# A decoder block on one core: the input product in passes over 512 features of h, with partial sums seeded back into PSUM

## The chip, the core and the metric

One core of a Trainium2 chip runs the whole kernel. The metric is the device time of one execution in microseconds (us), as the median of several runs. TensorE is PE in the profile, VectorE DVE, ScalarE ACT, GpSimd POOL; SyncE (SP) issues the DMAs.

## What is computed

One layer for 256 tokens (S) of 2,048 features (D), all in float32:

```python
mod = silu(c) @ w_ada + b_ada                      # 6 blocks of 2048: shift, scale, gate (mix), shift, scale, gate (ffn)
h = rmsnorm(x, g_pre_mix) * (1 + scale_m) + shift_m
z = h @ w_in                                       # q_lat, kv_lat, k_rope, gq, gk, gv, g_lr, g_og, gate_a, gate_b
y_a = mla_branch(...) @ w_branch_a                 # attention, 8 heads, latents up-projected, rope
y_b = gla_branch(...) @ w_branch_b                 # gated linear attention, 4 heads: a scan over tokens
merged = sigmoid(gate_a) * y_a + sigmoid(gate_b) * y_b
x = x + gate_m * rmsnorm(merged @ w_mix_out, g_post_mix)
h = rmsnorm(x, g_pre_ffn) * (1 + scale_f) + shift_f
x = x + gate_f * rmsnorm(conv_ffn(h), g_post_ffn)  # up to 2 x 5632, causal conv of width 3, gelu gate, down
```

The weights are 386 MB, read once. w_ada alone is 100 MB; the shift and scale of the first h are 4,096 of its 12,288 columns.

## The kernel before

**Numbers.** A float32 operand is split in a high part (float32r) and a low part, and a product is the sum of three matmuls: high x high, high x low, low x high. That holds for the weights and for h (`ht[:, k, 0]` and `[:, k, 1]`).

**Units, pairs, groups.** Weights come in *units* of 256 rows by 512 columns (512 KB, `raw`, a ring of 4). For each unit ScalarE makes the high half (`w_hi`, line 911), VectorE the low half (`w_lo`, line 1281), each one instruction of 128 x 1,024. TensorE takes two units at a time, a *pair*: 48 matmuls of 256 columns (`feature_pair`, lines 499 to 528) or 24 of 512. A *group* is 512 output columns: the pairs that sum over all of the rows (4 pairs for 2,048 rows) in two PSUM tiles (banks 0 to 3 rotate, `BANKS`), which ScalarE then copies out (`empty`, line 935). The list `GROUPS` (line 61) gives the order: misc (kv latent, rope, low-rank gate), qlat, gq x2, qup x3, kup, vup, gk x2, gv x4, og x4, ga x4, gb x4, ba x4, bb x4, mix x4, ffn x22, down x4, in all 530 units, 265 pairs, 133 of them before FFN.

**What sets the order.** Every engine's order is written out by hand; semaphores join them. ScalarE makes the high halves of pair k+2 once pair k is done (`pairs_used`, or `tile_ready` for the last pair of a group; `split_at`, line 922). The load of a unit waits on SP until the low half of the unit four back is made (line 314), and the one SP queue issues all of the loads in order.

**The modulation.** w_ada comes in units of 128 rows by 1,024 columns (512 KB, `ada`, a ring of 4). VectorE multiplies each by one column of silu(c) and adds it to `acc` (`ada_unit`, line 1284; 192 units in all). TensorE then sums `acc` over the partitions with a column of ones (`mod_columns`, line 567; for the first two blocks, lines 597 to 604). Shift and scale of the first h need 64 units; they run in two halves of 1,024 features (`first_ada`, lines 343 and 1362; `acc` and `acc_2`): after the first 32 units half of h is made (`input_hi`, line 968; `input_f` and `input_lo`, lines 1380 to 1391) and TensorE runs two pairs of misc, after the next 32 the rest. Then one unit of w_ada goes beside each pair, until the sixth block is done at the end of mix.

**Attention, scan.** From gk on, `mla_at` puts the pieces of a head of attention after the pairs, one head per two pairs (`scores`, `transpose_probs`, `context`); then come `gate_preact`, the decays (`log_gate`, `log_decay`) and 9 levels of the scan, one per two pairs: ScalarE's exponentials (`decays`, line 1079), VectorE's products (`products`, line 1520), TensorE's `level` (line 721), VectorE's masked copy (`select`, line 1528). GpSimd does the prefix sums (lines 1805 to 1814). The output of the scan (`gla_out`, `gla_norm_sum`) stands beside ga, one piece per pair. `gate_rows` (line 848) spreads the gate of the mix over all partitions after the last pair of ba; og_s, the split input of bb, is made when ba begins (lines 1150, 1618).

`pace` (line 495) is a small matmul ahead of a group.

Of the kernel before, what the change touches and what calls it, by code (L numbers as in the profile page):

```python
# [7 lines left out]
P = 128  # L8
# [52 lines left out]
GROUPS = ([("misc", 8, 2), ("qlat", 8, 2)] + [("gq", 8, 2)] * 2  # L61
          + [("qup", 2, 2)] * 3 + [("kup", 2, 4)] + [("vup", 2, 4)]
          + [("gk", 8, 2)] * 2 + [("gv", 8, 2)] * 4 + [("og", 8, 2)] * 4
          + [("ga", 8, 2)] * 4 + [("gb", 8, 2)] * 4 + [("ba", 4, 2)] * 4 + [("bb", 8, 2)] * 4
          + [("mix", 8, 2)] * 4 + [("ffn", 8, 2)] * 22 + [("down", 22, 2)] * 4)


def starts(name):

    u = t = p = 0  # L70
    a = 2 * ADA_BLOCK
    for kind, nu, nt in GROUPS:
        if kind == name:
            return u, t, p, a
        u, t, p = u + nu, t + nt, p + nu // 2 - 1
        if nu in (4, 8) and a < 6 * ADA_BLOCK:
            a += nu // 2
    return u, t, p, a


UNITS = starts("end")[0]
FIRST_OF = {g[0]: starts(g[0]) for g in GROUPS}


HALVES = {"mix": 0, "down": 8}
BANKS = 4

# [26 lines left out]
def build(nc, ap, out):  # L114
# [4 lines left out]
    with ctx:  # L119
# [41 lines left out]
        conv_a = at(5, "conv_a", [P, 4, S], F32, 4)  # L161
        conv_v = at(9, "conv_v", [P, 4, S], F32, 4)
# [9 lines left out]
        x_tok = at(B + 96, "x_tok", [P, NT, D], F32, 16)  # L172
        xn_tok = at(B + 112, "xn_tok", [P, NT, D], F32, 16)
        xn_t = at(B + 48, "xn_t", [P, KT, S], F32, 16)
        h_f = at(B + 64, "h_f", [P, KT, S], F32, 16)
# [8 lines left out]
        acc_2 = at(B + 128, "acc_2", [P, D], F32, 8)  # L184

        lat = at(B + 48, "lat", [P, 6, S], F32, 6)
        lat_s = at(B + 54, "lat_s", [P, 6, 2, S], F32R, 12)
        lat_sq = at(B + 66, "lat_sq", [P, 6, S], F32, 6)
        q_rope_in = at(B + 72, "q_rope_in", [P, 4, S], F32, 4)
        rope_tmp = at(B + 76, "rope_tmp", [P, 2, S], F32, 2)  # L190
        lat_r = at(B + 78, "lat_r", [P, 2, S], F32, 2)
# [11 lines left out]
        w_gate = at(B + 48, "w_gate", [P, GH * DK], F32, 4)  # L203
# [16 lines left out]
        brow_m = at(B + 128, "brow_m", [P, UC], F32, 2)  # L220
# [27 lines left out]
        tile_empty = sem("tile_empty")  # L248
        ada_used = sem("ada_used")
# [33 lines left out]

        def halves(t, h):
# [25 lines left out]
        def _(sp):  # L310
            def load_unit(u, r, src):
# [5 lines left out]
            def load_ada(a, r, src):  # L317

                if not isinstance(a, int) or a >= RING:
                    sp.wait_ge(ada_used, a - (RING - 1))  # L320
                sp.dma_start(ada[:, r], src).then_inc(ada_loaded[r], 16)

# [3 lines left out]
            def ada_src(block_no, kt, half):  # L326
                return w_ada[bass.ds(kt * P, P), bass.ds(block_no * D + half * AC, AC)]

            def group(u0, nu, src, a0=None, a_block=None, a_kt=None, slot0=0):

                for j in range(nu):
                    load_unit(u0 + j, (slot0 + j) % RING, src(j))
                    if a0 is not None and j % 2 == 1:
                        n = j // 2
                        load_ada(a0 + n, n % RING, ada_src(a_block, a_kt + n // 2, n % 2))

            def small(dst, src, loaded=rows_loaded):
                sp.dma_start(dst, src).then_inc(loaded, 16)

            def as_rows(v):  # L340
                return v.rearrange("(r c) -> r c", c=P)

            def first_ada(half, i):

                for r in range(RING):
                    a = 2 * KT * half + 4 * i + r
                    load_ada(a, r, ada_src(r % 2, 2 * i + r // 2, half))

            def load_misc(j):

                r = j % RING
                rs = w_in[j * 2 * P:(j + 1) * 2 * P, :].rearrange("(k p) n -> p k n", p=P)
                if j >= RING:
                    sp.wait_ge(lo_done, j - (RING - 1))
                sp.dma_start(raw[:, r, :, 0:320], rs[:, :, C_KV:C_KV + 320]).then_inc(raw_loaded[r], 16)
                sp.dma_start(raw[:, r, :, 320:384], rs[:, :, C_KR:C_KR + ROPE]).then_inc(raw_loaded[r], 16)
                sp.dma_start(raw[:, r, :, 384:512], rs[:, :, C_LR:C_LR + P]).then_inc(raw_loaded[r], 16)
# [7 lines left out]
            first_ada(0, 0)  # L365
            sp.dma_start(x_tok[:], x[0].rearrange("(t p) d -> p t d", p=P)).then_inc(x_loaded, 16)
# [9 lines left out]


            with sp.Fori(1, KT // 2) as i:
                first_ada(0, i)
            for j in range(RING):  # L380
                load_misc(j)
            with sp.Fori(0, KT // 2) as i:
                first_ada(1, i)
            _, _, _, a0 = FIRST_OF["misc"]
            for j in range(RING, 8):
                load_misc(j)
                if j >= RING + 1:
                    n = j - RING - 1
                    load_ada(a0 + n, n, ada_src(3, n // 2, n % 2))
            load_ada(a0 + 3, 3, ada_src(3, 1, 1))  # L390
            u0, _, _, a0 = FIRST_OF["qlat"]
            group(u0, 8, lambda j: two_kt(w_in, 256 * j, C_Q), a0, 3, 2)
            u0, _, _, a0 = FIRST_OF["gq"]
            with sp.Fori(0, 2) as g:
                group(u0 + 8 * g, 8, lambda j: two_kt(w_in, 256 * j, C_GQ + UC * g), a0 + 4 * g, 3, 4 + 2 * g)

            u0 = FIRST_OF["qup"][0]
            qv = w_q_up.rearrange("(k p) (h e) -> p k h e", p=P, e=NOPE + ROPE)
            for n in range(6):
                g, j = n // 2, n % 2  # L400
                r = (u0 + n) % RING
                sp.wait_ge(lo_done, u0 + n - (RING - 1))
                for k in range(2):
                    if g < 2:
                        dst = raw[:, r, k, :].rearrange("p (h e) -> p h e", h=4)
                        sp.dma_start(dst, qv[:, 2 * j + k, 4 * g:4 * g + 4, 0:NOPE]).then_inc(raw_loaded[r], 8 * 2)
                    else:
                        dst = raw[:, r, k, :].rearrange("p (h e) -> p h e", h=H)
                        sp.dma_start(dst, qv[:, 2 * j + k, :, NOPE:NOPE + ROPE]).then_inc(raw_loaded[r], 8 * 2)

            u0 = FIRST_OF["kup"][0]
            kvv = w_kv_up.rearrange("(k p) (h e) -> p k h e", p=P, e=NOPE + VD)
            for n in range(4):
                part, hh = n // 2, n % 2
                r = (u0 + n) % RING
                sp.wait_ge(lo_done, u0 + n - (RING - 1))
                for k in range(2):
                    dst = raw[:, r, k, :].rearrange("p (h e) -> p h e", h=4)
                    sp.dma_start(dst, kvv[:, k, 4 * hh:4 * hh + 4, part * NOPE:part * NOPE + P])\
                        .then_inc(raw_loaded[r], 16)  # L420
            s0 = FIRST_OF["gk"][0] % RING
            u0, _, _, a0 = FIRST_OF["gk"]
            with sp.Fori(0, 2) as g:
                group(u0 + 8 * g, 8, lambda j: two_kt(w_in, 256 * j, C_GK + UC * g), a0 + 4 * g, 3, 8 + 2 * g, s0)

            sp.wait_ge(tile_ready, FIRST_OF["gk"][1])
            sp.dma_start(w_gate[0:GR, :], w_gla_gate_up).then_inc(gate_w_loaded, 16)
            u0, _, _, a0 = FIRST_OF["gv"]
            with sp.Fori(0, 2) as g:
                group(u0 + 8 * g, 8, lambda j: two_kt(w_in, 256 * j, C_GV + UC * g), a0 + 4 * g, 3, 12 + 2 * g, s0)  # L430
# [11 lines left out]
            with sp.Fori(0, 2) as g:  # L442
                for n in range(2):
                    group(u0 + 8 * g + 4 * n, 4, lambda j: two_kt(w_branch_a, 256 * j, 2 * UC * g + UC * n),
                          None, None, None, s0)
                    for m in range(2):
                        load_ada(a0 + 4 * g + 2 * n + m, 2 * n + m, ada_src(2, 12 + 2 * g + n, m))
# [1389 lines left out]
```

## Time and profile before

| | us |
|---|---|
| median of three runs | 1787.48 |
| lowest and highest | 1781.24, 1788.38 |
| the profiled execution | 1779.35 |
| its span, from the first to the last instruction | 1777.6 |
| busy in it: PE, DVE, ACT, POOL | 1623.0, 1130.9, 749.6, 39.0 |
| mean DMA rate over the span | 219 GB/s |

PE's busy time is that of pipelined matmuls whose ends are modelled, so busy is not the same as at its peak. Times in rows are in us from the start of the span; a line of a timeline gives the start, the time that it took (for several of a kind, from the first to the last), engine, line of the kernel, operation and operands, and in brackets how long the engine had been idle and what ended that.

### The profile page before, as it was taken

The page shows a single profiled execution, that of the slowest core. Times are in us where ns is not written, and L with a number is a line of the kernel's source. Part 1 is how long each engine was busy: PE and PEld are TensorE (multiplying, and loading weights), DVE is VectorE, ACT ScalarE, POOL GpSimd, SP SyncE. Part 2 cuts the span into 40 slices and gives each one's busy share as a digit, 9 for nine tenths or more (in the row PEclk, how much of TensorE's full clock was granted, in tenths as well). Part 3 has the DMA queues.
Part 4 walks back from the last instruction along what each step waited for, and adds up shares of the span by engine and source line. Part 5 has one row for each costly group of instructions (what it writes and reads, how often), then busy time and mean ns, then how long its engine had stood idle before and what let it go on. Part 6 is the DMA issues. An engine that isn't in the chain of part 4 may idle for free.

```text
span 1777.6 us, 30678 instructions
## 1 busy us (share of the span) xinstructions
PE 1623.0 (91%) x11660; PEld 1509.6 (85%) x11660; DVE 1130.9 (64%) x1266; ACT 749.6 (42%) x921; POOL 39.0 (2%) x22
## 2 busy tenths in 40 slices
PE   1149999998998999998999789999999999999997
PEld 1149999787998999996988589999999999788886
DVE  6686756658775458684777756666666666544444
ACT  3114454435343454441443454455444455333332
POOL 0000000002220000000000000000000000000000
PEclk9569999998999999997999899999999999999999
DMA  8998867665565669983788636565566666555553
GB/s 310 330 308 294 235 217 233 229 214 185 172 212 178 213 214 297 298 289 134 265 314 294 226 112 192 187 192 190 189 189 191 195 193 195 170 190 190 190 191 138
DMA packets 188654, 389.15 MB, mean 219 GB/s; under 512 B 18445, under 2 KB 31503, under 8 KB 187815
## 3 DMA queue, kind: packets, MB, share of 16 engines
q1 hardware_dynamic: 188583, 388.17, 66.4%
q8 instruction: 48, 0.79, 0.2%
q14 instruction: 23, 0.19, 0.0%
HBM read 386.02 MB, written 2.10 MB: 218 GB/s over the span
## 4 chain that ended last, share of the span: by engine, by line
PE 81%; DVE 9%; DMA 4%; issue 3%; ACT 2%; SPq 1%; DVEq 0%; ACTq 0%
PE ps L519 17%; PE ps L521 17%; PE ps L523 17%; PE ps L558 6%; PE ps L560 6%; PE ps L559 6%; DMA ada<-in_w_ada 3%; DVE acc L1293 3%; DVE w_lo L1281 3%; PE ps L743 2%; ACT w_hi L911 1%; PE ps L795 1%; PE ps L797 1%; PE ps L796 1%; PE ps L855 1%
## 5 line engine op out<-in xcount | busy, mean ns | idle before, releaser
L1281 DVE TENSOR_TENSOR w_lo<-raw,w_hi 128x1024 fp32r<-128x1024 f32 x530 | 639.3, 1247 | 542.3 <-ACT w_hi L911 540.9
L911 ACT ACTIVATE w_hi<-raw 128x1024 fp32r<-128x1024 f32 x530 | 532.3, 1052 | 806.8 <-PE ps L523 521.9
L519 PE MATMUL ps<-h2t,w_hi 128*128 128x256 f32 x1408 | 390.7, 277 | 0.0
L523 PE MATMUL ps<-h2t,w_lo 128*128 128x256 f32 x1408 | 389.2, 276 | 0.0
L521 PE MATMUL ps<-h2t,w_hi 128*128 128x256 f32 x1408 | 389.1, 276 | 0.0
L519 PE MATMUL ps<-ht,w_hi 128*128 128x256 f32 x1152 | 329.4, 286 | 43.5 <-DVE ht L1391 40.1
L521 PE MATMUL ps<-ht,w_hi 128*128 128x256 f32 x1152 | 325.1, 282 | 0.0
L523 PE MATMUL ps<-ht,w_lo 128*128 128x256 f32 x1152 | 324.9, 282 | 0.0
L521 PEld LDWEIGHTS ps<-h2t,w_hi 128*128 128x128 f32 x1408 | 264.7, 188 | 0.0
L519 PEld LDWEIGHTS ps<-h2t,w_hi 128*128 128x128 f32 x1408 | 264.3, 188 | 0.0
L523 PEld LDWEIGHTS ps<-h2t,w_lo 128*128 128x128 f32 x1408 | 264.3, 188 | 0.0
L519 PEld LDWEIGHTS ps<-ht,w_hi 128*128 128x128 f32 x1152 | 223.5, 194 | 45.0 <-issue 41.0
L1293 DVE SCALAR_TENSOR_TENSOR acc<-ada,c_act,acc 128x1024 f32<-128x1024 f32 x182 | 234.1, 1293 | 19.9 <-DMA ada<-in_w_ada 19.0
L521 PEld LDWEIGHTS ps<-ht,w_hi 128*128 128x128 f32 x1152 | 223.1, 194 | 0.1
L523 PEld LDWEIGHTS ps<-ht,w_lo 128*128 128x128 f32 x1152 | 222.4, 193 | 0.0
L558 PE MATMUL ps<-w_hi,hid 128*128 128x512 f32 x352 | 138.8, 394 | 1.1 <-DVE w_lo L1281 1.1
L560 PE MATMUL ps<-w_hi,hid 128*128 128x512 f32 x352 | 137.8, 392 | 0.0
L559 PE MATMUL ps<-w_lo,hid 128*128 128x512 f32 x352 | 137.4, 390 | 0.0
L558 PEld LDWEIGHTS ps<-w_hi,hid 128*128 128x128 f32 x352 | 66.1, 188 | 16.2 <-DVE w_lo L1281 1.5
L560 PEld LDWEIGHTS ps<-w_hi,hid 128*128 128x128 f32 x352 | 66.1, 188 | 14.9
L559 PEld LDWEIGHTS ps<-w_lo,hid 128*128 128x128 f32 x352 | 66.1, 188 | 14.3
L519 PE MATMUL ps<-og_s,w_hi 128*128 128x256 f32 x256 | 72.7, 284 | 2.2 <-DVE w_lo L1281 2.2
(257 smaller groups left out, 1872.6 us busy)
## 6 DMA issues: line engine op xcount, KB each, us to landing
ada<-in_w_ada SPq DMA_DIRECT2D x192, 512.0 KB, 5.2
raw<-in_w_ffn_up SPq DMA_DIRECT2D x176, 512.0 KB, 4.5
raw<-in_w_in SPq DMA_DIRECT2D x168, 512.0 KB, 4.5
raw<-in_w_ffn_down SPq DMA_DIRECT2D x88, 512.0 KB, 3.8
raw<-in_w_branch_b SPq DMA_DIRECT2D x32, 512.0 KB, 5.5
raw<-in_w_mix_out SPq DMA_DIRECT2D x32, 512.0 KB, 5.5
raw<-in_w_branch_a SPq DMA_DIRECT2D x16, 512.0 KB, 5.9
raw<-in_w_q_up SPq DMA_DIRECT2D x12, 256.0 KB, 4.0
```

The source lines that it names most:

```text
L519: mm(o, w_hi[:, s, k, cols], moving[:, kt, 0], start=opens, stop=False, skip_group_check=True)
L521: mm(o, w_hi[:, s, k, cols], moving[:, kt, 1], start=False, stop=False, skip_group_check=True)
L523: ins = mm(o, w_lo[:, s, k, cols], moving[:, kt, 0], start=False, stop=stop, skip_group_check=True)
L558: mm(o, still[:, kt, 0, tok], w_hi[:, s, k, :], start=start, stop=False)
L559: mm(o, still[:, kt, 0, tok], w_lo[:, s, k, :], start=False, stop=False)
L560: ins = mm(o, still[:, kt, 1, tok], w_hi[:, s, k, :], start=False, stop=last and i == 1 and k == 1)
L743: ins = mm(o, lhs[:, d, keys], rhs, start=i == 0, stop=i == 1)
L795: mm(o, ht[:, kt, 0, tok], w_hi[:, s, k, :], start=first and i == 0 and k == 0, stop=False)
L796: mm(o, ht[:, kt, 0, tok], w_lo[:, s, k, :], start=False, stop=False)
L911: A(w_hi[:, slot], raw[:, slot], ACT.Copy).then_inc(hi_done, 1)
L1281: V.tensor_tensor(w_lo[:, slot], raw[:, slot], w_hi[:, slot].bitcast(F32), ALU.subtract)\
L1293: ins = V.scalar_tensor_tensor(part, ada[:, slot], c_act[:, bass.ds(kt, 1)], part, ALU.mult, ALU.add)
```

## The change

**Passes.** `PASSES` takes the place of `GROUPS`. The first 14 groups of w_in (FIRST: misc, qlat, gq, gq, gk; SECOND: gk, gv x4, og x4) no longer sum over all rows at once. One pass is one pair, 512 rows: all 14 over rows 0 to 511 (pairs 0 to 13), all 14 over rows 512 to 1,023 (14 to 27), then FIRST over rows 1,024 to 1,535 and 1,536 to 2,047 (28 to 37). After them come qup, kup, vup (38 to 42), and SECOND over its last 1,024 rows, two pairs a pass (43 to 60). From ga on (pair 61) the order is as before. The number of pairs is the same.

**Seeds.** At the end of a pass ScalarE copies the two tiles out to their place in SBUF as before. Ahead of the next pass over the same columns it copies them back into PSUM (`seed`), at the end of the pass two before, and the first matmul of that pass doesn't clear the bank (`opens` is false). TensorE waits for `seeded`.

**The modulation.** The first two blocks come in quarters: a unit is 128 rows by 512 columns of shift and the same of scale. 16 units make 512 features of h; TensorE starts pair 0 then. The other 48 units stand beside pairs 0 to 30, one or two each (`ada_schedule`), the columns and h's next quarter after pairs 11, 21 and 31. Blocks 2, 3, 4 follow beside pairs 33 to 51 and 65 to 77, 80 to 104, 106 to 130; block 5 beside the first eight FFN groups, through one slot. `acc_2` is gone.

**Attention and scan.** A head per pair from pair 43 (`MLA`), a level per pair from 57 (`GLA` is 55), the output of the scan from pair 65 (`OUT`), beside ga. The prefix sums are on VectorE (`scan`), in place of GpSimd. `gate_rows` comes after pair 79, columns of blocks 3 and 4 after 105 and 131. og_s is made after the last pair of ba (100). `pace` stays for gb, ba, bb and FFN, and is gone elsewhere.

The diff, cut:

```diff
+FIRST = [("misc", 0), ("qlat", 0), ("gq", 0), ("gq", 1), ("gk", 0)]
+SECOND = [("gk", 1)] + [("gv", g) for g in range(4)] + [("og", g) for g in range(4)]
+PASSES = ([(kind, g, 0, 2) for kind, g in FIRST + SECOND] + [(kind, g, 4, 2) for kind, g in FIRST + SECOND]
+          + [(kind, g, 8, 2) for kind, g in FIRST] + [(kind, g, 12, 2) for kind, g in FIRST]
+          + [("qup", g, 2, 2) for g in range(3)] + [("kup", 0, 0, 2), ("vup", 0, 0, 2)]
+          + [(kind, g, 8, 4) for kind, g in SECOND]
+          + [(kind, g, 0, 8) for kind in ("ga", "gb") for g in range(4)] + [("ba", g, 0, 4) for g in range(4)]
...
@@ SP @@
+            sp.dma_start(x_tok[:], x[0].rearrange("(t p) d -> p t d", p=P)).then_inc(x_loaded, 16)
+            for a in range(12):
+                load_ada(a)
+            load_pair(0)
+            for a in range(12, 16):
+                load_ada(a)
+            load_pair(1)
...
+            for k in range(FFN):
+                if k + 2 < FFN:
+                    load_pair(k + 2)
+                for n in range(ADA_AT[k]):
+                    load_ada(ADA_BEFORE[k] + n)
...
@@ PE @@
+                if seed is not None:
+                    pe.wait_ge(seeded, seed + 1)
+                elif not isinstance(t, int) or t >= 4:
                     pe.wait_ge(tile_empty, t - 3)
...
-                                opens = first and f == 0 and j == 0 and k == 0
+                                opens = first and seed is None and f == 0 and j == 0 and k == 0
...
+                if k in (11, 21, 31):
+                    first_columns((k - 1) // 10)
+                h = k - MLA
+                if 0 <= h < H:
+                    scores(h)
+                if 0 <= h - 3 < H:
+                    context(h - 3)
+                if 0 <= h - 2 < H:
+                    transpose_probs(h - 2)
...
+                if k == GLA:
+                    level(0)
+                if 1 <= k - GLA - 1 < LEVELS:
+                    level(k - GLA - 1)
...
@@ ACT @@
+            def seed(t, src):
+
+                act.wait_ge(tile_empty, t - 3)
+                A(as_tile(t, src), src, ACT.Copy).then_inc(seeded, 1)
...
+                else:
+                    split_pair(k + 2)
+                    if last and kind not in ("ba", "bb"):
...
+                        for b in range(2):
+                            empty(t0 + b, home(kind, g, b), ACT.Sigmoid if kind in ("ga", "gb") else ACT.Copy,
+                                  GLA_SCALE if kind == "gq" and k0 == 12 else 1.0)
+                        seed_pass(i + 2)
...
+                if kind == "ba" and g == 3 and last:
+                    act.wait_ge(og_gated, 4)
+                    act.wait_ge(tile_ready, first_tile("ba"))
+                    for q in range(4):
+                        A(og_s[:, 4 * q:4 * q + 4, 0], o_gla[:, 4 * q:4 * q + 4], ACT.Copy).then_inc(og_hi, 1)
...
@@ DVE @@
+            def scan(lv):
+
+                h = 1 << (lv - 1)
+                p0, p1 = halves(pre, h)
+                s0, _ = halves(suf, h)
+                dve.wait_ge(dec_ready, lv)
+                V.tensor_tensor(s0, s0, spread(p1[:, :, h - 1:h], s0), ALU.add).then_inc(suffix_ready, 1)
+                dve.wait_ge(suffix_ready, lv)
+                V.tensor_tensor(p1, p1, spread(p0[:, :, h - 1:h], p1), ALU.add).then_inc(scan_ready, 1)
...
+                if 1 <= k - GLA - 1 < LEVELS:
+                    select(k - GLA - 1)
+                if 1 <= k - GLA < LEVELS:
+                    if k - GLA < LEVELS - 1:
+                        scan(k - GLA)
+                    products(k - GLA)
...
+                for a in range(ADA_BEFORE[k], ADA_BEFORE[k] + ADA_AT[k]):
...
+                        ada_unit(a, a % RING, a % ADA_BLOCK // 2, a % 2, 16 * (a // RING + 1))
```

On VectorE these units come after the low halves and the small pieces of their pair, and ahead of the products of ba, bb and of og_s's low parts.

## Rows read from the trace of the kernel before

**Rows 1.** The page's 40 slices: TensorE's clock, then what the memory moved.

```profile
PEclk9569999998999999997999899999999999999999
GB/s 310 330 308 294 235 217 233 229 214 185 172 212 178 213 214 297 298 289 134 265 314 294 226 112 192 187 192 190 189 189 191 195 193 195 170 190 190 190 191 138
```

**Rows 2.** The page's chain of work that ended last, by engine.

```profile
PE 81%; DVE 9%; DMA 4%; issue 3%; ACT 2%; SPq 1%; DVEq 0%; ACTq 0%
```

**Rows 3.** Stretches: length, busy PE, PEld, DVE, ACT, POOL (count), clock, DMA share, GB/s.

```profile
640.00:760.00 120.00, 120.00 (x1060) 120.00 (x1060) 92.25 (x78) 56.96 (x60) 0.00 (x0) 1.00 0.87 286
1034.00:1512.00 478.00, 478.00 (x4202) 478.00 (x4202) 302.06 (x388) 238.10 (x304) 0.00 (x0) 1.00 0.60 189
```

**Rows 4.** Timeline of VectorE in the first 136 us.

```profile
37.49 2.67 DVE L1293 SCALAR_TENSOR_TENSOR acc<-ada,c_act,acc 128x1024 f32<-128x1024 f32 x2 [0.44 <-DMA ada<-in_w_ada]
...
125.49 1.28 DVE L1293 SCALAR_TENSOR_TENSOR acc<-ada,c_act,acc 128x1024 f32<-128x1024 f32 x1 [0.89 <-DMA ada<-in_w_ada]
...
134.39 1.23 DVE L1391 TENSOR_TENSOR ht<-h_f,ht 128x1024 fp32r<-128x1024 f32 x1 [0.72 <-ACT ht L973]
```

**Rows 5.** Timeline, TensorE's first matmul on h.

```profile
103.36 0.55 PE L519 MATMUL ps<-ht,w_hi 128*128 128x256 f32 x1 [29.98 <-DVE ht L1391]
```

**Rows 6.** Timeline of ScalarE: high halves, each pair of them behind a pair of TensorE.

```profile
143.23 2.01 ACT L911 ACTIVATE w_hi<-raw 128x1024 fp32r<-128x1024 f32 x2 [5.01 <-PE ps L523]
...
290.17 2.01 ACT L911 ACTIVATE w_hi<-raw 128x1024 fp32r<-128x1024 f32 x2 [1.08 <-PE ps L523]
...
304.36 2.01 ACT L911 ACTIVATE w_hi<-raw 128x1024 fp32r<-128x1024 f32 x2 [1.08 <-PE ps L523]
...
469.35 2.01 ACT L911 ACTIVATE w_hi<-raw 128x1024 fp32r<-128x1024 f32 x2 [6.76 <-PE ps L523]
...
484.93 2.01 ACT L911 ACTIVATE w_hi<-raw 128x1024 fp32r<-128x1024 f32 x2 [8.13 <-PE ps L523]
...
559.25 2.00 ACT L911 ACTIVATE w_hi<-raw 128x1024 fp32r<-128x1024 f32 x2 [5.01 <-PE ps L523]
...
574.03 2.01 ACT L911 ACTIVATE w_hi<-raw 128x1024 fp32r<-128x1024 f32 x2 [5.92 <-PE ps L523]
...
805.28 2.00 ACT L911 ACTIVATE w_hi<-raw 128x1024 fp32r<-128x1024 f32 x2 [3.43 <-PE ps L523]
...
834.84 2.01 ACT L911 ACTIVATE w_hi<-raw 128x1024 fp32r<-128x1024 f32 x2 [27.56 <-PE ps L523]
```

**Rows 7.** Chain in order of time: mod_columns, a selection, a level, gate rows twice.

```profile
367.08 3.47 PE ps L573 x32
...
474.00 1.23 DVE attn L1551 x8
475.37 3.76 PE ps L743 x32
...
810.07 2.05 PE ps L853 x2
...
1515.85 1.05 PE ps L855 x2
```

**Rows 8.** Groups by line and shape: count | busy us, mean ns | idle before.

```profile
L911 ACT ACTIVATE w_hi<-raw 128x1024 fp32r<-128x1024 f32 x530 | 532.3, 1052 | 806.8 <-PE ps L523 521.9 <-PE ps L560 185.3 <-DMA raw<-in_w_in 58.6
L939 ACT ACTIVATE k_gla<-ps 128x512 f32<-128x512 f32 x4 | 2.1, 584 | 0.0
L1281 DVE TENSOR_TENSOR w_lo<-raw,w_hi 128x1024 fp32r<-128x1024 f32 x530 | 639.3, 1247 | 542.3 <-ACT w_hi L911 540.9
```

**Rows 9.** Timeline of VectorE, two low halves while GpSimd scans.

```profile
439.50 5.29 DVE L1281 TENSOR_TENSOR w_lo<-raw,w_hi 128x1024 fp32r<-128x1024 f32 x2
```

**Rows 10.** DMA issues from 650 to 800 us: count, KB each, us to landing.

```profile
raw<-in_w_in SPq DMA_DIRECT2D x34, 512.0 KB, 4.9
```

More of the change, by code:

```diff
@@ new lines, in numbers @@
+def numbers():
+    first, tiles, seeds, pairs = [], [], [], []
+    t = p = n = 0
+    for i, (kind, g, k0, nu) in enumerate(PASSES):
+        nt = 4 if kind in ("kup", "vup") else 2
+        first.append((t, p))
+        seeded = k0 > 0 and kind != "qup"
+        seeds.append(n if seeded else None)
+        n += nt if seeded else 0
+        for m in range(nu // 2):
+            last = m == nu // 2 - 1
+            pairs.append((i, m, ("tile_ready", t + nt) if last else ("pairs_used", p + m + 1)))
+        t, p = t + nt, p + nu // 2 - 1
+        tiles.append(nt)
+    return first, tiles, seeds, pairs
@@ L85, with at_pair, first_tile @@
+START, TILES, SEEDS, PAIRS = numbers()
+def at_pair(kind, g=0, k0=None):
+    return next(k for k, (i, m, _) in enumerate(PAIRS)
+                if PASSES[i][:2] == (kind, g) and m == 0 and (k0 is None or PASSES[i][2] == k0))
+def first_tile(kind):
+    return START[PAIRS[at_pair(kind)][0]][0]
+UNITS = 2 * len(PAIRS)
+LAT = at_pair("qlat", 0, 12)
+MLA = at_pair("gk", 1, 8)
+GLA = MLA + 12
+OUT = MLA + 22
+ROWS = OUT + 14
+FFN = at_pair("ffn")
 HALVES = {"mix": 0, "down": 8}
 BANKS = 4
+GATE_BANKS = ((7, 4), (6, 5))
@@ new lines, in ada_schedule @@
+def ada_schedule():
+    n = [0] * FFN
+    for k in range(31):
+        n[k] = 2 if k % 2 == 0 or k == 15 else 1
+    for k in list(range(33, MLA + 9)) + list(range(OUT, ROWS - 1)):
+        n[k] = 1
+    for k in list(range(ROWS + 1, ROWS + 25)) + list(range(ROWS + 27, ROWS + 51)):
+        n[k] = 2 if k % 3 == 0 else 1
+    assert sum(n[:31]) == 48 and sum(n[31:ROWS]) == 32
+    assert sum(n[ROWS:ROWS + 25]) == 32 and sum(n[ROWS + 25:]) == 32
+    return n
+ADA_AT = ada_schedule()
+ADA_BEFORE = [16 + sum(ADA_AT[:k]) for k in range(FFN)]
@@ L89, in level_masks @@
+MOD_3 = ROWS + 26
+MOD_4 = FFN - 2
 def level_masks():
@@ L329, in group @@
[L329 to L357, printed above, removed]
+            qv = w_q_up.rearrange("(k p) (h e) -> p k h e", p=P, e=NOPE + ROPE)
@@ L390, in _ @@
[L390 to L409, printed above, removed]
@@ L439, in _ @@
-            sp.wait_ge(og_psum, 8)
-            sp.dma_start(gpost_m[:], g_post_mix[0:1, :].to_broadcast([P, D])).then_inc(post_loaded, 16)
-            u0, _, _, a0 = FIRST_OF["ba"]
[L442 to L447, printed above, removed]
@@ new lines, in _, with ffn_loads @@
+            u0, a0 = 2 * FFN, 5 * ADA_BLOCK
+            def ffn_loads(g, with_ada):
+                for part in range(2):
+                    for j in range(8):
+                        load_unit(u0 + 16 * g + 8 * part + j, (u0 + j) % RING,
+                                  two_kt(w_ffn_up, 256 * j, part * FF + UC * g))
+                        if with_ada and j in (3, 7):
+                            n = 2 * part + j // 4
+                            sp.wait_ge(ada_used, a0 + 4 * g + n)
+                            sp.dma_start(ada[:, 3], w_ada[bass.ds((2 * g + n // 2) * P, P), bass.ds(5 * D + n % 2 * AC, AC)])\
+                                .then_inc(ada_loaded[3], 16)
```

1247 lines of the change are left out of this document (541 added, 706 removed).

## The prediction

> **What bounds the kernel now.** I read the page's slices first, for the places where TensorE falls behind. TensorE runs at full clock from about 150 us on; in the first slices it is nearly idle at half clock, while the memory moves 290 to 330 GB/s [rows 1]. The chain agrees: 81% of it is TensorE, and the 4% of DMA and much of the 9% of VectorE lie at the start [rows 2]. The table by stretches gives the price of steady work: FFN's 88 pairs of units (two units, 48 matmuls of 256 columns) take 478 us, so **a pair costs 5.44 us** with TensorE never idle, and w_in's gate columns run at the same pace while 286 GB/s come in [rows 3]. So the kernel is 265 pairs of TensorE time plus what lies between them, and a change pays only in what lies between.
>
> The timeline of VectorE tells what the start is: it sums shift and scale columns as w_ada lands, the 16th unit being used by 40.2 us, the 64th by 126.8 us; then come the columns on TensorE and the split of h, whose low part ends at 135.6 us [rows 4]. TensorE's first two pairs ran at 103 to 111 and 118 to 124 us, after 30 us of nothing [rows 5]. ScalarE's high halves are a clock of the pairs, as each pair of them waits for the pair of units before last: pair 2 ended at 143.2 us [rows 6], 3 x 5.44 back is 126.9 us, the point from which the pairs would have run without a gap.
>
> **The start.** After the change 16 units of w_ada make the first 512 features of h, not 64. The same bytes have landed by then as at 40.2 us before, plus pair 0's 1 MB put in between (3.4 us at 310 GB/s, between slices of rows 1), in pieces of 2 KB where they were 4 KB, for which I add 1 us: the last of the 16 is used at 44.5 us. From 126.8 to 135.6 us the same tail took 8.8 us before; it has half of the columns now (16 of 32 instructions), so at half clock, where 32 take twice the 3.47 us of [rows 7], less 2 us and some: 7 us. TensorE starts at 51.7 us. The pair that starts cold took 7.6 us (135.6 to 143.2), I say 8: pair 0 ends at 59.8 us, and 5.44 back is 54.4. **Gain 126.9 - 54.4 = 72.5 us**, between 66 (two stalls of the ring) and 75.
>
> **Loads beside the first 31 pairs.** They carry 48 more units of w_ada: per pair 1.05 MB of weights and 1.55 x 0.52 MB, 1.86 MB, which at 5.44 us is 342 GB/s. The columns stretch moved 286 GB/s at a share of 0.87 [rows 3], so 329 at a full share, and 1.86 MB takes 5.66 us: 31 x 0.22 = 7 us. If it only reaches the 310 of the slices it is 31 x 0.56 = 17; if the stretch's share understates what is left, 0. **Cost 7 us.** The Trainium skill, page DMA: Bandwidth & Descriptors, section Specifications, gives HBM a limit of about 358 GB/s per core; by that figure the pair would stay at 5.44 us and this cost would be nothing. The trace has slices of 330 and none above, so its row is kept.
>
> **ScalarE beside those pairs.** A pass is one pair now: two high halves (2 x 1.05), two evictions (2 x 0.58) and two seeds [rows 8]. No row shows a copy into PSUM; the nearest are the eviction's 0.58 us for 512 elements and half of a 1.05 us copy of 1,024: I take 0.58; twice that is the dear bound. Sum 4.4 us, 5.6 us at the dear bound: under, or 0.1 over, the pair. As pass i seeds for i+2, one pair of TensorE covers it. VectorE has two low halves (2 x 1.25) and 1.55 sums (1.28): 4.5 us. **Nothing**, dear bound 5 us. Behind them on both queues are the chunks of h (four ScalarE pieces, two VectorE steps, three times): they have one to three pairs of cover. The three new sets of columns stand on TensorE's path: 16 instructions, 1.7 us each: **cost 5 us**.
>
> **Latents.** The chain from root to low part had a whole group of four pairs; it has two, and VectorE has splits and a sum ahead of its part. Nothing to one pair: **cost 3.5 us**.
>
> **Attention and scan beside one pair each.** A head had two pairs and cost 14.2 - 10.9 = 3.3 us (304.36 less 290.17 in [rows 6]); with one pair the round is 5.44 + 3.3 = 8.7 us, and no other engine has more than 7 us in it (VectorE: 2.5, 1.3 and some 2.7 of small pieces). Same cost. A level took 15.6 us in two pairs (484.93 less 469.35), 4.7 above them. Now: level 3.76 us, selection 1.23 us [rows 7], two scan steps and two products of 1,024 elements at 1.25 us, 5 us, all in a ring: 10.0 us, some 10.2 with semaphores, against 9.2 of TensorE: 4.8 above the pair; on ScalarE every second pair has evictions and seeds ahead of the decays, 1 us more in three or four levels. **Cost 4 us**, bounds 0 and 20. The scan leaves GpSimd; while it ran there, two low halves took 5.29 us against 2 x 1.25 [rows 8, 9], a delay that goes. The entry to the scan (gate, log, first decays: a long serial piece) keeps its length and I leave it equal.
>
> **Later.** (a) First output of the scan: 559.25 to 574.03 is 14.8 us [rows 6], a pair plus 1.4 is 6.8: the wait for the last selection has a pair of cover now, **gain 8**. (b) Gate rows: 805.28 to 834.84 us holds one pair and 24.1 us [rows 6]; 4.8 were a wait for the sums and eight steps ran at 2.05, which at full clock take 1.05 (the second such set) [rows 7]. Moved among the gate columns, with sums done two pairs ahead: 8.4 us, **gain 15.5**, at least 7.7 if at half clock. (c) og_s is split only after the last branch-a pair. Behind that pair: first high half, two low halves, one sum, two gate products (half of 1.25 each), one low part: 1.05 + 2.5 + 1.3 + 1.3 + 1.25 = 7.4 us, in which TensorE waits; then half clock for a while, 4; before, that place lost 1.3. **Cost 10**, bounds 6 and 15. (d) w_ada's last block beside FFN: two sums per four pairs (21.8 us) for VectorE, busy 302 of 478 us: nothing; if they delayed one split per group, 11 us. (e) A pace matmul and a rope wait less: gain 2.
>
> **Sum**: 72.5 - 7 - 5 - 3.5 - 4 + 8 + 15.5 - 10 + 2 = 68.5 us. The profiled execution took 1779.35 us (span 1777.6): 1710.9. The median of three is 1787.5, 8 above it; I put half of that on top: **1714 us**.
>
> **Rivals.** (1) *Loads and ScalarE bind more*: the first stage's period is 6.4 to 7 us, or the scan's ring 12 to 13: 25 to 45 us less gain, 1740 to 1760. For it: every copy is now serial behind a pair; against: margins of 1 us above. Chance 0.2. (2) *Slower*: landing time. Pair k+2 is issued when pair k's low halves are made, 2 periods less 3.5 us before it is due; w_ada's queue turns behind it in the same in-order queue. Landing took 4.9 us at 290 GB/s [rows 10]; 7.4 us decide whether there is a loss, and from (L + 3.5)/2 = 7.7 us, L = 11.9, the change is slower. With L = 14: 8.75 us, 31 x 3.3 = 103 us, 1806 us. 0.05. (3) *The clock falls in single-pair passes*. From 440 us on TensorE changed banks and waited a little each level and the slices show 9 tenths or more [rows 1]. The Trainium skill, TensorE: Matmul & The Clock Gate, section A second HAM failure mode, says that cycling through PSUM banks with micro-idles makes the clock swing. As a mechanism of this kernel, with half of 31 pairs at half clock: 15 x 5.44 = 82 us, 1796: no change. 0.03. (4) *The start is not where the time is*: x's own chain (norm, transposes) ends after the 16th unit. x is now first in the queue, so it would have to lose 10 us: 1724, inside the range. The forecast has the rest, 0.72.
>
> **Numbers.** The range takes in the forecast with its bounds (1695 to 1735) and most of rival 1: 1692 to 1758. About 0.5% is what a measurement of this kernel tells from no change. Faster 0.92, the same 0.03, slower 0.05.
>
> **What would show it.** First TensorE pair near 52 us; high halves every 5.5 to 5.8 us up to 230 us, with the memory above 310 GB/s; heads every 8.7, levels every 10.2; gate rows in 8.4 us; one wait of 7 us at the first branch-b matmul; FFN unchanged at 478 us. A wait of TensorE on ScalarE's copies into PSUM in the first stage, or a period above 6.5 us there, would prove the forecast wrong.

## The result and the profile after

The changed kernel takes 1824.1 us (median of four runs, 1819.4 to 1831.3) against 1785.7 us before on the same chip: a ratio of 1.022, 95% interval 1.018 to 1.026. It is 2.2% slower where 1714 us was forecast. The profiled execution, the slowest of the four, took 1831.27 us; its span is 1829.5 us.

The page of the kernel after, slices and chain (the lines that answer to [rows 1, 2]):

```profile
PEclk8899999998999899899979898989898999999999
GB/s 290 274 326 337 322 236 228 219 153 93 109 207 246 178 318 312 228 247 344 324 160 116 173 171 197 165 210 148 197 171 173 191 187 195 163 193 192 194 187 138
...
PE 71%; DVE 9%; DMA 7%; issue 5%; ACT 5%; SPq 1%; DVEq 0%; ACTq 0%
PE ps L544 14%; PE ps L546 14%; PE ps L548 14%; PE ps L573 7%; PE ps L571 7%; PE ps L572 7%; DMA raw<-in_w_ffn_up 6%; ACT w_hi L890 3%; DVE w_lo L1232 3%; PE ps L730 2%; DVE acc L1266 2%; DVE acc L1255 1%; DMA ada<-in_w_ada 1%; DVE conv_v L1626 1%; DVE hid_f L1639 1%
```

TensorE's share of the chain fell by ten points, and a DMA stands in it that was not there: the landing of w_ffn_up's raw units, 6% of the span, some 110 us. At the start the clock's slices read 8 and 8 where they read 5 and 6. New are five dips, in every second slice from the 23rd to the 31st, which lie in FFN; the kernel before has none there.

Where the time went is told by TensorE's first and last matmul of FFN. The trace's group of `w_lo` matmuls on `h2t`, of the kernel before and then of the one after (name, count, duration min/median/max in ns, first and last start in us):

```profile
L523 PE MATMUL ps<-h2t,w_lo x1408: 276/276/286, 1033.1 to 1514.7; 128*128 128x256 f32 x176
```

```profile
L548 PE MATMUL ps<-h2t,w_lo x1408: 276/276/416, 964.5 to 1565.7; 128*128 128x256 f32 x176
```

FFN begins 68.6 us earlier and lasts 601.2 us where it lasted 481.6: 119.6 us more. Behind it the two are alike (262.9 us to the end of the span before, 263.8 after). So -68.6 + 119.6 + 0.9 = +51.9, which is the difference of the spans. The forecast's sum, 68.5 us, is there at the door of FFN; all of the miss is inside.

FFN as a whole, before and then after (columns as in [rows 3]):

```profile
1032.80:1514.80 482.00, 482.00 (x4235) 482.00 (x4236) 304.29 (x390) 239.21 (x305) 0.00 (x0) 1.00 0.59 188
```

```profile
964.20:1565.80 601.60, 525.55 (x4235) 522.15 (x4236) 342.84 (x422) 242.96 (x305) 0.00 (x0) 0.93 0.52 178
```

For the same 4,235 matmuls TensorE is busy 43.6 us longer, at a clock of 0.93, and idle for 76.0 us: that is the whole of the 119.6.

Two stretches inside (the first lies in the eight groups with w_ada's last block, the second is mostly the three groups without it):

```profile
965.00:1432.00 467.00, 390.95 (x3076) 387.55 (x3075) 257.25 (x313) 177.57 (x222) 0.00 (x0) 0.91 0.50 175
1432.00:1550.00 118.00, 118.00 (x1016) 118.00 (x1017) 76.05 (x99) 57.90 (x76) 0.00 (x0) 0.98 0.60 188
```

Without w_ada FFN keeps the old pace. With it, TensorE idles 76 of 467 us at a clock of 0.91, and every other engine is less busy than before too, the memory with them (175 GB/s, share 0.50, against 189 and 0.60 in [rows 3]): nobody works at a limit, somebody waits. Who, the trace's waits of that stretch show, TensorE's, ScalarE's, VectorE's and SyncE's queue (who waited <- for what: us in total, times, longest):

```profile
PE ps L544 <- DVE w_lo L1232: 42.4, 9, 6.1
PE ps L522 <- DVE w_lo L1232: 33.6, 8, 4.8
...
ACT w_hi L890 <- DMA raw<-in_w_ffn_up: 158.6, 51, 9.7
...
DVE w_lo L1232 <- ACT w_hi L890: 201.7, 55, 8.2
...
SPq L482 <- DVE acc L1266: 379.4, 31, 33.1
```

Read backwards: TensorE waits for low halves, 17 times; VectorE for high halves; ScalarE for the raw units to land; and the queue that issues the raw units stands 379 of 467 us in front of one semaphore, "the previous unit of w_ada has been summed" (line 481, then the DMA of line 482). The timeline of SyncE's queue shows it as bunches:

```profile
980.17 0.34 SPq L482 DMA_DIRECT2D ada<-in_w_ada  x1
980.77 2.23 SPq L371 DMA_DIRECT2D raw<-in_w_ffn_up  x4
991.82 0.35 SPq L482 DMA_DIRECT2D ada<-in_w_ada  x1
992.41 2.23 SPq L371 DMA_DIRECT2D raw<-in_w_ffn_up  x4
1008.65 0.35 SPq L482 DMA_DIRECT2D ada<-in_w_ada  x1
1009.56 2.24 SPq L371 DMA_DIRECT2D raw<-in_w_ffn_up  x4
```

Four raw units are issued at once each time, and only when a sum is done. The chain at the first of these:

```profile
978.73 1.29 DVE acc L1266
980.17 0.34 SPq L482
980.77 0.37 SPq L371
981.39 6.71 DMA raw<-in_w_ffn_up
988.11 1.06 ACT w_hi L890
989.20 1.24 DVE w_lo L1232
990.44 0.12 issue
990.56 0.58 PE ps L544
991.13 0.21 PE ps L546
```

From the end of the sum (980.0) to the landing at 988.1 no unit is in the ring: the ring of four has run dry. TensorE still has its last pair until 986.2; then it idles for 4.35 us, until the new unit has landed and been split (990.6). Its matmuls then come every 0.21 us, which is half clock; from 994.1 on they come every 0.12 us again.

**Theory A** from these rows. In a group of 16 units VectorE sums behind units 7, 9, 15 and 17 (`j in (5, 7)` of both parts; 17 is unit 1 of the next group). SyncE loads w_ada behind raw units 3, 7, 11 and 15, always into slot 3, and each load waits for the sum before it. The load behind raw unit 7 needs the sum that stands behind the low half of unit 7 (and 15 that of 15). Raw units 8 to 11 stand behind it in the same queue, though their own slots (those of 4 to 7) come free one by one from unit 4 on. So twice in each of eight groups all four slots run empty. 119.6 / 16 = 7.5 us each: 4.75 us of waiting (76.0 us, in 17 recorded waits) and 2.7 us of slower matmuls. **Rivals**: B, VectorE overfull with the sums; C, the added transfers make the units land late; D, a loss of pace that has nothing to do with w_ada. (The expectations say 107 us: they took FFN to end at 1550, before I had the last matmul's row. The right figure is 119.6.)

### The profile page after: what moved, and what is told of

It is laid out like the page before. It is cut to its first block, busy times and chain, and to the rows that moved or that the text cites. A ratio compares the mean times of both kernels' runs of the same rounds, so it can differ in the third digit from the quotient of the medians.

```text
span 1829.5 us, 29229 instructions
## 1 busy us (share of the span) xinstructions
PE 1658.2 (91%) x11650; PEld 1548.2 (85%) x11650; DVE 1131.3 (62%) x1285; ACT 819.7 (45%) x1053; POOL 3.7 (0%) x9
## 4 chain that ended last, share of the span: by engine, by line
PE 71%; DVE 9%; DMA 7%; issue 5%; ACT 5%; SPq 1%; DVEq 0%; ACTq 0%
PE ps L544 14%; PE ps L546 14%; PE ps L548 14%; PE ps L573 7%; PE ps L571 7%; PE ps L572 7%; DMA raw<-in_w_ffn_up 6%; ACT w_hi L890 3%; DVE w_lo L1232 3%; PE ps L730 2%; DVE acc L1266 2%; DVE acc L1255 1%; DMA ada<-in_w_ada 1%; DVE conv_v L1626 1%; DVE hid_f L1639 1%
## 5 line engine op out<-in xcount | busy, mean ns | idle before, releaser
L1232 DVE TENSOR_TENSOR w_lo<-raw,w_hi 128x1024 fp32r<-128x1024 f32 x530 | 627.1, 1222 | 615.6 <-ACT w_hi L890 614.0
L544 PE MATMUL ps<-h2t,w_hi 128*128 128x256 f32 x1408 | 409.9, 291 | 42.4 <-DVE w_lo L1232 42.4
L546 PE MATMUL ps<-h2t,w_hi 128*128 128x256 f32 x1408 | 406.1, 288 | 0.0
L548 PE MATMUL ps<-h2t,w_lo 128*128 128x256 f32 x1408 | 405.4, 288 | 0.0
L544 PEld LDWEIGHTS ps<-h2t,w_hi 128*128 128x128 f32 x1408 | 281.1, 200 | 44.2 <-issue 43.4
L546 PEld LDWEIGHTS ps<-h2t,w_hi 128*128 128x128 f32 x1408 | 281.4, 200 | 0.0
L548 PEld LDWEIGHTS ps<-h2t,w_lo 128*128 128x128 f32 x1408 | 280.3, 199 | 0.0
```

Of the source, the lines that this page charges most:

```text
L544: mm(o, w_hi[:, s, k, cols], moving[:, kt, 0], start=opens, stop=False, skip_group_check=True)
L546: mm(o, w_hi[:, s, k, cols], moving[:, kt, 1], start=False, stop=False, skip_group_check=True)
L548: ins = mm(o, w_lo[:, s, k, cols], moving[:, kt, 0], start=False, stop=stop, skip_group_check=True)
L1232: V.tensor_tensor(w_lo[:, slot], raw[:, slot], w_hi[:, slot].bitcast(F32), ALU.subtract)\
```

## Experiments on FFN

The kernel before ran beside every experiment, at 1791 to 1792.5 us in the median where it had 1785.7 beside the first runs; the ratios to it are the safer figures.

**Without the block.**

```diff
-                        if with_ada and j in (3, 7):
-                            n = 2 * part + j // 4
-                            sp.wait_ge(ada_used, a0 + 4 * g + n)
-                            sp.dma_start(ada[:, 3], w_ada[bass.ds((2 * g + n // 2) * P, P), bass.ds(5 * D + n % 2 * AC, AC)])\
-                                .then_inc(ada_loaded[3], 16)
...
-                        if with_ada and j in (5, 7):
-                            n = 2 * part + (j - 5) // 2
-                            ada_unit(a0 + 4 * g + n, 3, 2 * g + n // 2, n % 2, 16 * (a0 // RING + 4 * g + n + 1))
...
-            gate_rows(6 * ADA_BLOCK, brow_f)
+            gate_rows(5 * ADA_BLOCK, brow_f)
```

> Leaves out w_ada's last block beside FFN altogether: its 32 loads and its 32 sums, so the gate row of FFN is made of the bias alone. The time it gives is that of the kernel after without this work. Changed kernel: 1824 us median, FFN 965 to 1550 us. Every theory that puts the 107 us into this block (A: SyncE's in-order queue stands behind the one-slot buffer; B: VectorE is overfull with the sums; C: the memory serves the units later because of the added transfers) expects FFN in 478 us and 1824 - 107 = 1717 us. Theory D, that FFN lost its pace for another cause (the clock, which was at 1.00 there before and shows 0.91 now, or the state in which the ring of units enters FFN), expects no change: 1824 us.

Measured: 1712.0 us, ratio 0.954 (0.951 to 0.958). FFN, by the same row as above, 961.8 to 1447.5: 485.7 us. D falls: all but 4 us of the loss hangs on this block.

**Sums without loads.**

SyncE's five lines are out as above, and

```diff
-                            ada_unit(a0 + 4 * g + n, 3, 2 * g + n // 2, n % 2, 16 * (a0 // RING + 4 * g + n + 1))
+                            ada_unit(a0 + 4 * g + n, 3, 2 * g + n // 2, n % 2, 16 * (a0 // RING))
```

> Leaves out the 32 loads of w_ada's last block, keeps its 32 sums on VectorE at their places; they read what lies in the slot. A (the queue) and C (the transfers): as without the block, 1717 us, FFN 478 us. B (VectorE): all of the loss stays, 1824 us. If a part of the loss is that the two sums stand between low halves (32 x 1.28 us = 41 us of VectorE), it would show as a time between.

Measured: 1710.3 us, ratio 0.956 (0.952 to 0.960), FFN 484.6 us. The 32 sums cost VectorE 41 us of its time and the kernel nothing. B falls, and with it the only cost that the prediction had put on this edit.

**Loads with tiny sums.** Waits and order stay.

```diff
-                            ada_unit(a0 + 4 * g + n, 3, 2 * g + n // 2, n % 2, 16 * (a0 // RING + 4 * g + n + 1))
+                            dve.wait_ge(ada_loaded[3], 16 * (a0 // RING + 4 * g + n + 1))
+                            dve.wait_ge(ada_used, a0 + 4 * g + n)
+                            few = slice(n % 2 * AC, n % 2 * AC + 8)
+                            V.scalar_tensor_tensor(acc[:, few], ada[:, 3, 0:8], c_act[:, bass.ds(2 * g + n // 2, 1)],
+                                                   acc[:, few], ALU.mult, ALU.add).then_inc(ada_used, 1)
```

> Keeps the 32 loads, SyncE's waits and their order, but each sum covers 8 columns and not 1,024, so most of the gate row of FFN is left out. A: SyncE still stands behind the one slot until the sum behind unit 7 (15) of a group has run, only 1.2 us earlier each: 16 bubbles of 7 us less 1.2 are 93 us, so 1810 us, at least 1795. B: 1717 us. C: 1824 us.

Measured: 1802.4 us, ratio 1.008 (1.005 to 1.010). FFN runs from 966.0 to 1533.6: 567.6 us, 86.0 above the kernel before, where A had 93 (16 x (7.5 - 1.2) = 101 with the right figure). B had no loss here and falls a second time. C had all of it, 1824 us; it lies 22 us off, but weaker forms of C are left to the next run. SyncE's row of waits is nearly the old one:

```profile
SPq L482 <- DVE acc L1656: 344.3, 31, 32.0
```

**The same work, evenly spaced.** A's own test: SyncE's program is untouched.

```diff
+            ada_unit(a0, 3, 0, 0, 16 * (a0 // RING + 1))
...
-                        if with_ada and j in (5, 7):
-                            n = 2 * part + (j - 5) // 2
+                        if with_ada and j in (5, 9) and not (with_ada == "last" and part and j == 9):
+                            n = 2 * part + (j - 5) // 4 + 1
```

> The same work, the same 32 loads at the same places of SyncE's queue, the same 32 sums, but VectorE takes them one for every four units (behind units 3, 7, 11, 15 of a group) where it took them behind units 7, 9, 15, 17: each sum now runs before SyncE comes to the wait for it. A: the bubbles go, FFN 478 to 482 us, 1717 to 1722 us. B and C: nothing changes in the amount of work or of bytes, so 1824 us. A weaker form of C (landing 5.8 us and not 4.5) would leave 10 to 30 us of the 107.

Measured: 1714.2 us, ratio 0.956 (0.951 to 0.960); again, beside the kernels with doubled seeds and with both later steps:

> The kernel with the even spacing again, beside the next one on one chip, in five rounds, since the steps of 5 us after it are smaller than the 7 us by which the first runs spread. Expected 1712 us, ratio to the kernel before 0.956.

1714.0 us, 0.9565 (0.9535 to 0.9595). The first of them in rows, FFN's matmuls, the stretch of FFN, then SyncE's queue in two views:

```profile
L548 PE MATMUL ps<-h2t,w_lo x1408: 275/276/286, 963.5 to 1449.1; 128*128 128x256 f32 x176
```

```profile
965.00:1440.00 475.00, 475.00 (x4143) 475.00 (x4142) 336.19 (x416) 235.13 (x301) 0.00 (x0) 1.00 0.67 222
```

```profile
SPq L371 <- DVE w_lo L1232: 319.5, 168, 5.4
SPq L482 <- DVE acc L1264: 27.2, 1, 27.2
SPq L482 <- DVE acc L1266: 17.6, 30, 0.6
```

```profile
979.22 0.35 SPq L482 DMA_DIRECT2D ada<-in_w_ada  x1
982.29 6.95 SPq L371 DMA_DIRECT2D raw<-in_w_ffn_up  x4
990.07 0.34 SPq L482 DMA_DIRECT2D ada<-in_w_ada  x1
993.19 7.30 SPq L371 DMA_DIRECT2D raw<-in_w_ffn_up  x4
```

FFN takes 485.6 us with as many loads, sums and bytes as in the changed kernel. TensorE is never idle, at full clock, and the memory moves 222 GB/s where it moved 175. C falls; the raw units land in 4.5 us in the median, as before the change, where they took 6.6 with four issued at once. SyncE's waits for the sums shrank from 379 to 45 us, 27.2 of them a single wait at the first sum of the block; what it mostly waits for now is the low half that frees a raw slot, as a queue that feeds a ring should, and four raws are spread over 7 us where they came in 2.2. The Trainium skill, page Perfetto Trace Analysis, section Optimization Strategy, reads the same gap repeated on the saturated engine as a possible lack of buffers for the next tile. Here the gap repeated sixteen times; the trace agrees that the buffer is where to look, but not that more are needed: one slot is enough when its uses stand four units apart.

**Queue or late unit?** In the changed kernel two things are late, the raws behind the wait and the w_ada unit itself. This run keeps VectorE's places and moves SyncE's second load of each half behind raw unit 10.

```diff
-                        if with_ada and j in (3, 7):
-                            n = 2 * part + j // 4
+                        if with_ada and ((with_ada != "end" and (j == 3 or (part, j) == (1, 2)))
+                                         or (with_ada != "first" and (part, j) == (0, 2))):
+                            n = {(0, 2): -1, (0, 3): 0, (1, 2): 1, (1, 3): 2}[part, j]
```

> The changed kernel with VectorE's places as they are (sums behind units 7, 9, 15, 17), but SyncE issues the second load of each half group 3 units later in its queue, behind raw unit 10 and not behind unit 7, so that its wait for the first sum no longer stands ahead of raw units 8 to 10. What of the 107 us is the queue, and what is the load of w_ada itself that comes too late for the sum behind unit 9? It is issued when the first sum ends in both kernels, about 8 us before it is needed with 6.7 us of landing. If the raw units behind the wait are the loss (A in the narrow sense): 1717 us, up to 1740 where raw unit 11 is a little late. If the late w_ada unit holding VectorE is the loss: 1800 to 1824 us. C: 1824 us.

Measured: 1731.8 us, ratio 0.968 (0.965 to 0.971); FFN 962.6 to 1460.2, 497.6 us, 12 above the even spacing. That lies in what A in the narrow sense expected (1717 to 1740 us). Its waits in FFN, TensorE's and VectorE's (line numbers are 5 higher):

```profile
PE ps L549 <- DVE w_lo L1237: 7.0, 8, 1.4
...
DVE acc L1271 <- DMA ada<-in_w_ada: 24.4, 15, 2.3
```

VectorE does wait for the w_ada unit, 15 times some 1.6 us, and TensorE waits 7.0 us in all for low halves, where it waited for none with the even spacing. By these traces the 119.6 us are 103.6 for the raws held up in the queue (601.2 less 497.6), 12.0 for the uneven places themselves (497.6 less 485.6), and 4.0 that stay even without the block. Each of these is one execution: FFN took 483.6 to 488.7 us in the six traces that have the even spacing, so the 4.0 have no cause shown. By the ratios to the kernel before (1.022, 0.968, 0.956, 0.954, of some 1790 us) the same three parts are 97, 21 and 2 us. The order of size is the same, and the queue has four fifths or more. Two uses of the slot only two units apart are a small cost; what stands behind the wait for the first of them is a large one.

## Experiments on the other terms

**Copies into PSUM.** The prediction had no row for a seed and took 0.58 us. On top of the even spacing:

```diff
-                A(as_tile(t, src), src, ACT.Copy).then_inc(seeded, 1)
+                own.mark(A(as_tile(t, src), src, ACT.Copy))
+                own.wait()
+                A(as_tile(t, src), src, ACT.Copy).then_inc(seeded, 1)
```

> The kernel with the even spacing, each seed copied into PSUM twice, the second copy behind the first one's end: ScalarE gets 2 x 0.6 us and two waits more in each seeded pair. ScalarE has 4.0 us in such a pair and idles 1.67 us of 5.65. Theory (the prediction's: copies into PSUM lie beside one pair of TensorE and cost nothing): the time stays, 1714 us, at most 5 us more. Rival: the seeds bind already through ScalarE's queue (the 5.65 us period of pairs 12 to 21, where the others take 5.44): each seeded pass takes 0.6 to 1.2 us more, 24 passes, so 1728 to 1743 us.

Measured: 1711.6 us, ratio 0.956 (0.953 to 0.959), beside 0.9565 without. Twice the seeds cost nothing that shows. In the kernel after, two of them took 1.12 us, and TensorE waited for none:

```profile
225.67 2.01 ACT L890 ACTIVATE w_hi<-raw 128x1024 fp32r<-128x1024 f32 x2 [1.45 <-PE ps L548]
227.58 1.06 ACT L917 ACTIVATE lat<-ps 128x512 f32<-128x512 f32 x2
228.53 1.12 ACT L922 ACTIVATE ps<-q_gla 128x512 f32<-128x512 f32 x2
231.11 2.01 ACT L890 ACTIVATE w_hi<-raw 128x1024 fp32r<-128x1024 f32 x2 [1.45 <-PE ps L548]
```

**The split of og_s, spread.** On top of the even spacing: one quarter behind each of the pairs from the second branch-a group on (`q = k - at_pair("ba", 1)`, `0 <= q < 4`), on both engines.

> The kernel with the even spacing, and the split of og_s taken out of the last branch-a pair: one of its four high and low parts behind each of four pairs, the second to the fifth group's, where ScalarE idles 2.4 us and VectorE about 1 us in a pair. The working is the same in all else. If the prediction's term (c) is right in kind, the wait of TensorE at the first branch-b matmul (738.8 to 754.5 us in the changed kernel, one pair and 10.2 us) goes: 10 us off the even spacing's 1714 us, so 1704; bounds 8 and 13 (what VectorE's four low parts of 1.2 us may give back beside pairs in which it is full: up to 2 us). The rival: that the late place only looks costly and VectorE, with one and a half sums a pair beside the branches, is full there, so the split costs as much where it goes: 1714 us.

Measured: 1708.6 us, ratio 0.953 (0.950 to 0.957). In the kernel after TensorE stood still at this place, then started at half clock (timeline of TensorE):

```profile
745.91 0.39 PE L522 MATMUL ps<-og_s 128*128 128x64 f32 x1 [7.17 <-issue]
746.11 0.56 PE L544 MATMUL ps<-og_s,w_hi 128*128 128x256 f32 x1
```

With the split spread, the last branch-a matmul starts at 737.7 and the first on og_s at 737.9: the wait is gone. FFN starts at 949.6 instead of 963.2 us, 13.6 earlier; 2.0 of that were there before this place (the first branch-a matmul starts at 693.8 instead of 695.8), and FFN itself lasted 3 us longer in this execution. The medians differ by 5.6 us, less than the 8 to 13 expected, and the intervals of the two ratios overlap: the rows show that the wait is gone, but how much the split alone gives is not shown.

**The Silu, cut in two.** Also on top: `if n in (12, 13)`, half of `og` each, where it was one instruction at `n == 11`.

> As the run with the og_s split spread, and in addition the Silu of og (one ScalarE instruction of 3.64 us with a table load of 1.28 us behind the gate's two evictions and their own table load) is cut in two halves, behind the next two pairs, where nothing is evicted. Theory: in the changed kernel the high halves behind pair 75 start 3.8 us late (600.9 us), TensorE stands about 7 us, runs the next pair at half clock (5 us more) and the gate rows at half clock (11.7 us and not 8.4): 10 to 15 us to be had, so 1704 - 12 = 1692 us. Rival: the gate rows themselves throw the clock down, whatever is ahead of them: only the 7 us of waiting come back, 1697 us. Rival two: the halves stall the next two pairs as much: 1704 us.

Measured: 1704.5 us, ratio 0.952 (0.949 to 0.955), and again beside the even spacing:

> The kernel with the even spacing, the og_s split spread over four pairs and the Silu cut in two, again, beside the kernel with the even spacing alone. If both later steps are worth what their traces show (12 to 13 us less between the gate rows and FFN, 5 us less up to the gate rows), it is 12 to 17 us faster than the first in this call; if the rest of the time swings with the clock, 5 to 10 us.

1700.2 us, 0.949 (0.946 to 0.952), against 1714.0 for the even spacing beside it: 13.8 us for both steps together (expected 12 to 17), and FFN starts 14.0 us earlier (950.8, 964.8). The Silu's part was forecast too high. By the medians it was worth 4 us, not 10 to 15, and the intervals overlap here too. TensorE's wait there was 1.8 us, not the 7 that I had read out of the distance between high halves (which holds half-clock pairs as well). With the Silu cut TensorE waits for nothing between 580 and 650 us, so rival two, that the halves stall the next pairs as much, falls although its 1704 us was met. And the half clock beside the gate rows does not hang on the Silu. Stretch 600 to 625 us (columns as above, clock third from last) in two executions of the even spacing (Silu whole), and then in two with the Silu cut:

```profile
600.00:625.00 25.00, 23.17 (x101) 14.00 (x100) 15.57 (x14) 6.62 (x7) 0.00 (x0) 0.78 0.57 189
```

```profile
600.00:625.00 25.00, 23.17 (x132) 16.82 (x131) 15.57 (x14) 8.69 (x7) 0.00 (x0) 0.93 0.59 199
```

```profile
600.00:625.00 25.00, 25.00 (x164) 18.93 (x164) 15.88 (x15) 11.26 (x10) 0.00 (x0) 1.00 0.59 189
```

```profile
600.00:625.00 25.00, 25.00 (x123) 17.44 (x122) 12.77 (x12) 7.09 (x6) 0.00 (x0) 0.80 0.55 186
```

0.78 and 0.93, 1.00 and 0.80: the same kernel gives either, and the nine traces with the Silu whole span 0.77 to 1.00. The first branch-a matmul, behind this place, starts at 695.8 and 693.1 us in the first two and at 687.4 and 691.1 in the others, so some 3 to 4 us differ between executions of one kernel. Why was not pursued.

The last kernel beats both: 5% under the kernel before, 7% (0.949 against 1.022) under the changed one.

## Why the prediction was wrong, and where it was right

**The step that failed is (d) of "Later".** It priced w_ada's last block by VectorE's sums alone ("two sums per four pairs ... busy 302 of 478 us: nothing; if they delayed one split per group, 11 us"). The sums were indeed free. What the edit moved was also 32 loads into SyncE's in-order queue, each with a wait on a single slot, ahead of raw units; that wait was not counted, nor what stands behind it. The code gave it all: sums behind units 7 and 9, a wait behind raw unit 7. The walk through the queue would have shown the ring of four dry, 16 times. With the landing of 4.9 us [rows 10] left open each time it is 16 x 4.9 = 78 us of waiting, which would have taken the forecast from 1714 to about 1792, no change. Measured: 76.0 us of waiting, and 43.6 of slower matmuls behind it. That 78 is so near 76 is partly luck: at the first of these places the issue, a landing of 6.7 us and the two splits take 10.6 us, of which TensorE's last pair covers 6.2. Rival 2 had named w_ada's place in the in-order queue, but for the first 31 pairs, where four slots turn and TensorE waited for nothing.

**The sum up to FFN** was 68.5 against 68.6 measured, which is better than its parts:

- *The start*: pair 0 ended at 61.25 us (forecast 59.8); its first matmul stood at 52.59 (forecast 51.7).
- *Loads beside 31 pairs*: pair 30 ended at 231.11 (above). 61.25 + 30 x 5.44 + two sets of columns at 1.7 make 227.9, so 3.2 us and not 7, and none of it a wait for the memory. The first stage moved 306 to 330 GB/s at shares of 0.89 to 0.95; the page's highest slice is 344. The Trainium skill's limit of about 358 GB/s per core (page DMA: Bandwidth & Descriptors, section Specifications) holds for these stretches, but shorter ones go over it. The first of these rows lies in the first stage, the second where four raw units were issued at once in FFN; here the measurement decides, and 358 GB/s is not a ceiling for this kernel:

```profile
140.00:155.00 15.00, 15.00 (x130) 15.00 (x129) 11.53 (x10) 10.92 (x17) 0.00 (x0) 1.00 1.00 361
994.00:1000.00 6.00, 6.00 (x53) 6.00 (x53) 2.43 (x5) 1.98 (x3) 0.00 (x0) 1.00 1.01 383
```

- *The clock in single-pair passes* (rival 3) did not fall:

```profile
60.00:125.00 65.00, 65.00 (x476) 60.87 (x475) 48.17 (x42) 36.25 (x51) 0.00 (x0) 1.00 0.89 306
125.00:180.00 55.00, 55.00 (x423) 52.88 (x422) 43.67 (x43) 38.00 (x58) 0.00 (x0) 1.00 0.95 330
```

TensorE changes banks every pair here, and is busy all the time at 1.00. The rule of the page TensorE: Matmul & The Clock Gate, section A second HAM failure mode, in the Trainium skill, needs micro-idles; these rows have no idle, so they do not contradict it.

- *Latents*: one wait of 3.1 us (forecast 3.5). *Entry to the scan*, left equal in the forecast: TensorE waits 6.9 us, where it waited 3.4 and 1.9. *Heads* every 8.58 us (forecast 8.7), *levels* every 9.8 (forecast 10.2).
- *Gate rows*: from 586.24 to 629.05 us there are four pairs (21.8 us) and 21.0 us more, where 8.4 was forecast. The 12.6 us between hold a wait of 1.8 us behind the Silu, and pairs and gate rows at half clock; they were not taken apart further.
- *og_s*: 738.83 to 754.49 us holds a pair and 10.2 us. Forecast 10.
- *The shift and scale columns* of the FFN modulation moved from before the branches (366.9 to 630.5 us) to beside branch b and mix (776.1 to 934.9). The prediction left them out. The stretch from the first matmul on og_s to FFN grew from 206.5 to 218.1 us (826.3 to 1032.8; 746.1 to 964.2), 11.6 us.
- Against the misses at the gate rows and the columns stands that the first branch-a matmul came 65.3 us earlier (694.5 for 759.8), where the terms up to there give 54.6 (72.5 - 7 - 5 - 3.5 - 4 + 8 + 2 - 8.4), less the 12.6. Of the 23 us by which that is better than the terms, the moved columns are about 7 (two sets of 3.47 [rows 7]), the loads 3.8, the levels some 3; about 9 have no name. The agreement of the sum is luck in part.

**What the prediction said would show it wrong** (a wait on seeds, a first-stage period over 6.5 us) did not come. What failed is "FFN unchanged at 478 us", in the stage that the prediction had looked at least.

## What to carry to other kernels

When loads move into another queue position, walk the queue and not the engine: for each wait that a moved load brings, ask which later load stands behind it and whether the thing it waits for is done before that load's own slot comes free. A single slot is no fault, but two uses too close together are: keep the distance between a slot's uses at least the distance between its loads, and let each use precede the queue's wait for it. And price a dry ring as issue, landing and split, less the work that the engine still has in hand, plus what the clock takes afterwards; here the slower matmuls (43.6 us) came to more than half of the wait (76.0).

## What the runs showed of the hardware

- Stalls of 4.5 us in the mean, 17 of them in 467 us, went with a granted clock of 0.91 over the stretch, and 43.6 us of the loss are beside the 76.0 of waiting. With the waits gone FFN ran at 1.00, and also with eight waits of at most 1.4 us (7.0 in all, the run with the moved loads).
- With even spacing the nine pairs between 129.45 and 180.22 us took 5.64 us each where those from 203.91 to 236.55 took 5.44, at a clock of 1.00 both times and with TensorE waiting for nothing. ScalarE writes into PSUM in both stretches, and with each seed written twice the first still took 5.64 (129.96 to 180.73). What causes it is open; it is 2 of the 3.2 us above.
- ScalarE's copy from SBUF into PSUM took 0.60 us for 128 x 512, the copy out 0.58: the direction costs nearly nothing.
